# The first feed-forward matrix by seven products a block, its output through DRAM, the second matrix in four groups

## The reference

```
h = h + jnp.concatenate([y_rw, y_fox], axis=-1) @ w_out[i]     # 2048 x 2048
u = rmsnorm(h, norm_mlp[i])
h = h + jnp.square(jax.nn.relu(u @ w_ff1[i])) @ w_ff2[i]       # 2048 x 8192, 8192 x 2048
gate = jax.nn.sigmoid(rmsnorm(h, norm_ple[i]) @ w_ple_gate[i])
```

## Time and profile before

| stretch, us | what | PE busy | DVE busy | ACT busy | POOL busy |
|---|---|---|---|---|---|
| 1008 to 1095 | output projection, second half | 87.0 | 49.3 | 35.1 | 23.6 |
| 1095 to 2488 | the two feed-forward matrices | 1392.9 | 494.4 | 331.4 | 22.7 |
| whole span 2702.8 | | 2625.3 (97%) | 1232.4 (46%) | 896.8 (33%) | 192.4 (7%) |

### The profile page before, as it was taken

One profiled execution on the slowest core, in us unless ns is written; L12 is line 12 of the kernel. 1 busy time (PEld: TensorE's weight loads), 2 busy tenths in 40 slices (PEclk: granted clock), 3 DMA queues, 4 the chain that ended last, 5 costly groups with the idle time before them and its releaser, 6 DMA issues.

```text
span 2702.8 us, 45881 instructions
## 1 busy us (share of the span) xinstructions
PE 2625.3 (97%) x17810; PEld 2130.0 (79%) x17810; DVE 1232.4 (46%) x1638; ACT 896.8 (33%) x1338; POOL 192.4 (7%) x219
## 2 busy tenths in 40 slices
PE   7999999999688999999999999999999999999998
PEld 5777777777577678888888888888888888888887
DVE  5566676666644555443223442234422344334443
ACT  4443444444456324222122221222212122233333
POOL 0000000000233002000000000000000000011100
PEclk9999999999899999999999999999999999999999
DMA  7555444555523333333333333333333333333333
GB/s 201 152 153 162 141 141 143 164 162 149 189 87 105 112 99 95 99 100 94 94 100 93 101 94 95 99 93 101 93 96 98 94 100 93 98 96 107 95 97 105
DMA packets 524569, 310.26 MB, mean 115 GB/s; under 512 B 56501, under 2 KB 500903, under 8 KB 523495
## 3 DMA queue, kind: packets, MB, share of 16 engines
q1 hardware_dynamic: 475063, 265.15, 34.3%
q0 software_dynamic: 9264, 31.04, 3.3%
q10 hardware_dynamic: 40192, 13.40, 1.8%
HBM read 273.24 MB, written 36.31 MB: 115 GB/s over the span
## 4 chain that ended last, share of the span: by engine, by line
issue 53%; PE 35%; DVE 4%; ACT 3%; DMA 2%; POOL 1%; SPq 1%; POOLq 0%; DVEq 0%; ACTq 0%
PE acc L578 7%; PE acc L580 7%; PE acc L579 7%; PE acc L985 2%; PE acc L987 2%; PE acc L986 2%; ACT w_hi L1147 1%; POOL sumsq L2126 1%; PE bank L766 1%; PE acc L776 1%; PE bank L776 1%; DVE pr L1710 1%; PE bank L795 1%; DVE mx L1712 1%; PE bank L786 1%
## 5 line engine op out<-in xcount | busy, mean ns | idle before, releaser
L1581 DVE TENSOR_TENSOR w_lo<-w_raw,w_hi 128x1024 fp32r<-128x1024 f32 x420 | 521.5, 1242 | 1111.3 <-ACT w_hi L1147 1110.4
L1147 ACT ACTIVATE w_hi<-w_raw 128x1024 fp32r<-128x1024 f32 x420 | 444.5, 1058 | 1149.3 <-PE acc L580 1111.7
L578 PE MATMUL acc<-a_hi,w_hi 128*128 128x512 f32 x1824 | 719.9, 395 | 2.2 <-DVE w_lo L1581 2.1
L580 PE MATMUL acc<-a_hi,w_lo 128*128 128x512 f32 x1824 | 711.0, 390 | 0.0
L579 PE MATMUL acc<-a_lo,w_hi 128*128 128x512 f32 x1824 | 710.8, 390 | 0.0
L578 PE MATMUL acc<-b_hi,w_hi 128*128 128x512 f32 x1280 | 498.4, 389 | 0.0
L579 PE MATMUL acc<-b_lo,w_hi 128*128 128x512 f32 x1280 | 497.9, 389 | 0.0
L580 PE MATMUL acc<-b_hi,w_lo 128*128 128x512 f32 x1280 | 497.9, 389 | 0.0
L578 PEld LDWEIGHTS acc<-a_hi,w_hi 128*128 128x128 f32 x1824 | 342.8, 188 | 98.0 <-issue 22.4
L580 PEld LDWEIGHTS acc<-a_hi,w_lo 128*128 128x128 f32 x1824 | 342.8, 188 | 72.0
L579 PEld LDWEIGHTS acc<-a_lo,w_hi 128*128 128x128 f32 x1824 | 343.0, 188 | 71.6 <-issue 1.9
(11 more groups left out here) (297 smaller groups left out, 2032.9 us busy)
## 6 DMA issues: line engine op xcount, KB each, us to landing
w_raw<-in_w_ff SPq DMA_DIRECT2D x256, 512.0 KB, 4.0
w_raw<-in_w_in SPq DMA_DIRECT2D x100, 512.0 KB, 3.8
w_raw<-in_w_out SPq DMA_DIRECT2D x32, 512.0 KB, 4.1
w_raw<-in_w_ple_gate SPq DMA_DIRECT2D x32, 512.0 KB, 4.0
z_d<-ev POOLq DMA_DIRECT2D x50, 256.0 KB, 3.5
x_c<-ab_d SPq DMA_DIRECT2D x8, 1024.0 KB, 4.9
ab_d<-ab ACTq DMA_DIRECT2D x7, 1024.0 KB, 7.2
x_t<-ab_d SPq DMA_DIRECT2D x9, 512.0 KB, 3.6
```

Source lines behind the costliest of these rows:

```text
L578: mm(dst, wh, hi[:, kt, :], start=kt == 0, stop=False)
L580: last = mm(dst, wl, hi[:, kt, :], start=False, stop=kt == KT - 1)
L1147: A(w_hi[:, s, :, :], w_raw[:, s, :, :], ACT.Copy).then_inc(sg("w_hi_ready"), 1)
L1581: V.tensor_tensor(w_lo[:, s, :, 0:width], w_raw[:, s, :, 0:width], w_hi[:, s, :, 0:width].bitcast(F32), ALU.subtract).then_inc(sg("w_split ...
```

## The change

The first matrix (2048 x 8192) is cut into blocks of two by two: the input features in even and odd tiles of 128 (a = 0, 1), the tokens in two halves of 256, the hidden features in pairs of tiles of 128. Such a block product is made with seven products instead of eight. For that

- the normed input is kept as seven combinations (`mix`: a11, a12, s4, s1, s3, s2, a22, where s1 to s4 are sums of the four quarters), each of 256 tokens with high and low part side by side in one row of 512;
- of the weights the three blocks b11, b21, b22 and the four sums t1, t3, t2, t4 are used; GpSimd makes the sums, 1024 elements on each partition (`sum_weights`);
- a product is eight steps of two matmuls: w_hi with the row of 512 (high and low at once), w_lo with the 256 columns of the high part. VectorE reads the bank adding its two halves (`take_product`, a reduction), and adds up the seven results to the two output tiles;
- weights have four slots in place of two, and all seven other PSUM banks hold products;
- a finished pair of hidden tiles is squared by ScalarE and stored to DRAM (`hid_d`), 512 KB; `h` is stored too and reloaded after the first matrix, since `mix` takes its place;
- then the second matrix runs alone, in four groups of 16 tiles, each over a quarter of the hidden features; the next quarter is loaded and split during the group before.

32 pairs take the place of 64 tiles. The split of the input for the seven combinations is made in the output projection's second half: four 256-element sums of each pair of tiles on GpSimd, three copies on ScalarE, three residues on VectorE.

```diff
@@ TensorE
-            tiles(M_FF, 2, b_hi, b_lo, ready=2 * KT, beside=lambda u: spread_sumsq(1) if u == 1 else None)
-            tiles(M_FF + 2, KT - 2, b_hi, b_lo)
-            tiles(M_FF + KT, KT, a_hi, a_lo, ready=3 * KT)
-            with pe.Fori(0, FG - 1) as g:
-                tiles(M_FF + 2 * KT, KT, b_hi, b_lo, outer=g * (2 * KT))
-                tiles(M_FF + 3 * KT, KT, a_hi, a_lo, ready=g * KT + 4 * KT, outer=g * (2 * KT))
+            def seven_products(i, p, first=False):
+                for u in range(UNITS):
+                    wh, wl = slots[slot_of[u]]
+                    dst = product_banks[u]
+                    pe.wait_ge(sg("w_split"), i * UNITS + (FIRST + UNITS * p + u + 3))
...
+                    elif u % 2 == 0:
+                        pe.wait_ge(sg("products_taken"), i * 4 + (past("products_taken") + 4 * p - 3 + u // 2))
+                    for j in range(UK):
...
+                        mm(dst[:, :], wh[:, j, :], mixed(u, j), start=j == 0, stop=False, skip_group_check=True)
+                        last = mm(dst[:, 0:HT], wl[:, j, :], mixed(u, j)[:, 0:HT], start=False, stop=j == NJ, skip_group_check=True)
+                    last.then_inc(sg("unit_done"), 1)
...
+            seven_products(0, 0, first=True)
+            with pe.Fori(0, PAIRS - 1) as i:
+                seven_products(i, 1)
...
+            gemm(acc[0][:, :], *streams[0], Z_ODD + 2 * M_FF2, by_pair=2 * KT)
...
+            gemm(acc[1][:, :], *streams[0], Z_ODD + 2 * M_FF2 + 2)
+            tiles(M_FF2 + 2, KT - 2, *streams[0])
+            for g in range(1, FG):
+                tiles(M_FF2 + g * KT, KT, *streams[g % 2], ready=2 * KT + g * KT)
@@ SyncE
+            for q in range(4):
+                load_staged(q)
...
+            second_units(0, 0, 0)
+            for q in range(4, UK):
+                load_staged(q)
+            sp.wait_ge(sg("relu_ready"), past("relu_ready") + PAIRS)
+            sp.wait_ge(sg("hidden_stored"), past("hidden_stored") + 16 * PAIRS)
+            second_units(0, 0, 1)
+            stage_hidden(1, 0)
@@ VectorE
+            def product_lo(i, p, u):
+                dve.wait_ge(sg("w_hi_ready"), i * UNITS + (FIRST + UNITS * p + u + 1))
+                hi, lo = slots[slot_of[u]]
+                V.tensor_tensor(lo, weights_of[u], hi.bitcast(F32), ALU.subtract).then_inc(sg("w_split"), 1)
+            def take_product(dst, u):
+                return V.reduce_sum(dst, product_banks[u].rearrange("p (a t) -> p t a", a=2), AX.X)
...
+            def sums_4(i, p):
+                await_product(i, p, 6)
...
+                take_product(pq[1], 6).then_inc(sg("products_taken"), 1)
+                taken(i, p, 4)
+                then(V.tensor_tensor(ev[:, :, HT:T], pq[3][:, None, :].broadcast_to([P, 2, HT]), tile_sums[:, 1:3, :], ALU.add))
...
+                V.scalar_tensor_tensor(sq[:, :, :], ev[:, :, :], 0.0, rstd[:, None, :].broadcast_to([P, 2, T]), ALU.max, ALU.mult).then_inc(
+                    sg("relu_ready"), 1)
@@ GpSimd
+            def sum_weights(i, p):
+                b11, b12 = parts[:, 0, :, 0:P], parts[:, 0, :, P:]
+                b21, b22 = parts[:, 1, :, 0:P], parts[:, 1, :, P:]
+                t1, t3, t2, t4 = (tsum[:, n, :, :] for n in range(4))
+                def room(n):
+                    if p:
+                        pool.wait_ge(sg("w_split"), i * UNITS + (FIRST + UNITS * (p - 1) + n + 6))
...
+                G.tensor_tensor(t1, b12, b11, ALU.subtract).then_inc(sg("weight_sums_made"), 1)
...
+                G.tensor_tensor(t3, b22, b12, ALU.subtract).then_inc(sg("weight_sums_made"), 1)
...
+                G.tensor_tensor(t2, b22, t1, ALU.subtract).then_inc(sg("weight_sums_made"), 1)
...
+                G.tensor_tensor(t4, b21, t2, ALU.subtract).then_inc(sg("weight_sums_made"), 1)
```

More of the change, by code:

```diff
@@ L110, in sg @@
     def sg(name):
+        name = AGAIN[name][0] if name in AGAIN else name
         if name not in sems:
@@ L521, in _ @@
                     unit(b, w_out_v[:, 0:UK, bass.ds(i * (2 * P) + b * P, P)], i * 2 + (Z_ODD + 2 * M_OUT + KT + b))
[L522 to L530, removed]
+            ff1_parts = w_ff1.rearrange("l (k a p) n -> p (l a) k n", p=P, a=2)
@@ new lines, in _ @@
+            second_units(0, 0, 0)
[5 more added lines that the diff above has]
+            stage_hidden(1, 0)
+            for g in range(FG):
+                i0 = 1 if g == 0 else 0
+                with sp.Fori(0, KT // 2 - i0) as i:
+                    second_units(g, i, 0, i0)
+                    if g < FG - 1:
+                        stage_hidden(g + 1, i, i0)
+                    second_units(g, i, 1, i0)
@@ L1484, in _, with scale_tile @@
                     what(n)
[L1485 to L1492 removed]
+            def scale_tile(i, f0, b):
+                f = i * 2 + (f0 + b) if not isinstance(i, int) else f0 + b
+                act.wait_ge(sg("h_ready"), f + (KT + 1))
+                act.wait_ge(sg("mix_split"), i * 3 + (past("mix_split") + 3 * (f0 // 2)))
+                A(ev[:, b:b + 1, :], h[:, bass.ds(f, 1), :], ACT.Copy, scale=pc("norm_mlp", f)).then_inc(sg("tile_scaled"), 1)
@@ new lines, in _ @@
+            product_hi(0, 0, 0, first=True)
+            product_hi(0, 0, 1, first=True)
+            scale_tile(0, 2 * NJ, 1)
+            mix_his(0, NJ, 0)
+            product_hi(0, 0, 2, first=True)
+            square_tile(0, 2 * NJ, 1)
+            mix_his(0, NJ, 1)
+            mix_his(0, NJ, 2)
+            for u in range(3, UNITS):
+                product_hi(0, 0, u, first=True)
+            root(1)
+            with act.Fori(0, PAIRS - 2) as i:
+                for u in range(5):
+                    product_hi(i, 1, u)
+                square_hidden(i, 0)
+                for u in range(5, UNITS):
+                    product_hi(i, 1, u)
@@ L1510, in prepare @@
+                return body
+            for g in range(FG - 1):
+                stage(M_FF2 + g * KT, KT, body=next_hidden(g + 1))
+            stage(M_GATE - KT, KT, body=lambda i, b: fold(g_hi_all, "norm_ple", 2 * i + b, 2 * i + (b + 2 * KT), b))
             def prepare():
@@ new lines, in _, with to_last_lo @@
+            sums_76(0, 0)
+            product_lo(0, 1, 1)
+            def to_last_lo(i, p, last):
+                product_lo(i, p, 2)
+                product_lo(i, p, 3)
+                last()
+                product_lo(i, p, 4)
+                sums_12(i, p)
+                product_lo(i, p, 5)
+                product_lo(i, p, 6)
+            to_last_lo(0, 1, lambda: sums_4(0, 0))
+            with dve.Fori(0, PAIRS - 2) as i:
+                end = chained(i, 2)
+                sums_35(i, 1)
+                product_lo(i, 2, 0)
+                sums_76(i, 1)
+                product_lo(i, 2, 1)
+                to_last_lo(i, 2, lambda: sums_4(i, 1))
@@ L2240, in _ @@
+            sum_weights(0, 0)
+            with pool.Fori(0, PAIRS - 1) as i:
+                sum_weights(i, 1)
+            pool.wait_ge(sg("unit_done"), FIRST + 2 + UNITS * PAIRS)
+            for n in range(2):
+                pool.dma_start(h2[:, n * UK:(n + 1) * UK, :], h_v[:, n * UK:(n + 1) * UK, :]).then_inc(sg(f"h2_landed{n}"), 16)
+            for n in (2, 3):
                 sums(n)
```

439 lines of the change are left out of this document (353 added, 86 removed).

## The result

The changed kernel takes 2775.05 us (median of four runs, 2773.11 to 2777.12) where the kernel before takes 2704.4 in the same session: ratio 1.0258, 95% interval 1.0244 to 1.0273, 70 us slower. The forecast was 2765 us, range 2695 to 2830. The profiled execution has a span of 2773.8 us, 71.0 more than before.

The account below looks back on a forecast made before the run. VectorE and GpSimd, excluding each other at the SBUF port, were to bound the first matrix at 22.6 us a pair. -696.4 + 723.2 + 14 + 8 + 13 = +61.8 us on 2702.8 gave 2765 us, range 2695 to 2830.

Parts of the forecast that it names:

- likeliest case: Whole kernel: VectorE and GpSimd exclude each other, pair 22.6 us, total 2765 us, own range 2735 to 2800; chance 0.62.
- TensorE 19.4 us a pair as a floor: First matrix: seven products of 2.78 us make a 19.4 us pair, 75 us less in all if all else hides.
- A: Rival, first matrix: GpSimd's sums hide, TensorE stays the bound, pair 19.4 us, total 2650 us; chance 0.13.
- B: Rival, first matrix: narrow matmul doesn't halve because of its weight load, pair 24.8 us, total 2832 us; chance 0.06.
- D: Rival, first matrix: phases fall well, pair about 20.6 us, total within some 10 us of today; chance 0.06.
- The port, 6.3 us a pair: First matrix: of GpSimd's 9.6 us of sums 3.3 are covered; 6.3 add to VectorE's 16.3, pair 22.6 us.
- residues with a mean near 1.9 us: Sign of being right, first matrix: VectorE's weight residues have a mean near 1.9 us instead of 1.24.
- Rival C: First matrix: GpSimd keeps the port over consecutive sums while VectorE waits, pair 24.1 us, total 2824 us; chance 0.13.
- 8 was booked: First pair of the first matrix: weight sums start late, 8 us over an ordinary pair, ends 3 and 15.
- Projection, 14 us: Output projection's second half: chain of 12.9 us against TensorE's 10.9, 2.0 us booked seven times, ends 0 and 28.
- Handover, 13 us: Start of second matrix: late second-tile weights, wait 10.1 us, some 3 before the first tile; ends 5 and 20.
- Reloading the rows lies beside that: Handover to the second matrix: reloading rows, 5.9 us a megabyte, 2 MB first, lies beside the other waits.

Follow-up runs that it names:

- run 1: Changed kernel with GpSimd's four weight sums cut to 8 elements instead of 1024 from the second pair on; 2686.7 us, ratio 0.9931 to the kernel before.
- run 4: Changed kernel with three 256-column matmuls a step, VectorE copying 256 elements from the bank instead of reducing 512; 2747.97 us, ratio 1.0159 to the kernel before.
- run 7: Changed kernel with the second matrix's second weight tile requested before the wait for the last hidden pair's store; 2769.37 us, ratio 1.0239 to the kernel before.
- run 8: Run 7 with the reload of h issued later and VectorE waiting for it only at the first addition; 2765.23 us, ratio 1.0224 to the kernel before.
- run 5: Run 4 with VectorE adding straight from the product banks, weight sums kept on GpSimd; 2695.41 us, ratio 0.9961 to the kernel before.
- run 3: Changed kernel with the four weight sums made by VectorE instead of GpSimd from the second pair on; 2738.9 us, ratio 1.0126 to the kernel before.
- run 9: Changed kernel with ScalarE's weight copies ahead of scaling and mixing in the output projection's second half; 2763.95 us, ratio 1.0219 to the kernel before.
- run 6: Run 5 with the weight sums made by VectorE from the second pair on; 2695.26 us, ratio 0.9963 to the kernel before.
- run 2: Changed kernel with each weight sum replaced by two GpSimd fills of 1024 elements from the second pair on; 2685.31 us, ratio 0.9926 to the kernel before.

## Why the prediction was right

Its likeliest case came true, by its mechanism; that the pair agrees so closely, and the total within 10 us, is in part luck, as the steps show:

- **TensorE 19.4 us a pair as a floor.** The wide matmul starts a narrow one after 233 ns, the narrow one the next after 117, where 227 and 120 were taken. With nothing in its way (run 1) a pair takes 19.79 us. Rivals A, B and D are out: A needed the sums to hide, B a narrow matmul of 215 ns, D a pair of 20.6 us.
- **The port, 6.3 us a pair.** From the groups above: three residues (1.968 - 1.223), one L2347 (2.666 - 0.693), one L2320 (1.537 - 0.425), one L2329 (1.185 - 0.426) make 2.2 + 2.0 + 1.1 + 0.8 = 6.1 us of waiting a pair. Own work 16.3 was forecast, 22.56 - 6.1 = 16.5 measured, 0.3 of it idle. A sum that met nothing took 2.40 us, as taken from the rows, not 2.2. The pair of 22.6 was met to 0.04 us. What was wrong is where it waits: "residues with a mean near 1.9 us" holds for three of seven, and there as the mean of one of 3.4 and two of 1.2; 3.9 us of the 6.1 sit on additions of 256 and 512 elements, which I had not named. The cover was placed wrongly too. The forecast had reads of PSUM beside the four sums for 0.6, 1.2, 0 and 1.2 us; in the trace it is 0.2 (t1), 1.2 (t3), 1.4 (t2) and 0 (t4). Errors of over 1 us cancel, 3.0 against 2.8: that is luck. And the place can matter: in run 4 the same sums beside shorter reads cost more than before.
- **Rival C's mechanism is real, and its price shows only at the start.** In the first pair all four sums are ready to run one behind the other:

```profile
1120.90 2.36 POOL L2668 TENSOR_TENSOR tsum<-parts 128x1024 f32<-128x1024 f32 x1
1122.08 7.88 DVE L2296 TENSOR_TENSOR w_lo<-tsum,w_hi 128x1024 fp32r<-128x1024 f32 x2 [3.69 <-ACT w_hi L1677]
1123.21 2.35 POOL L2671 TENSOR_TENSOR tsum<-parts,tsum 128x1024 f32<-128x1024 f32 x1
1125.72 3.15 POOL L2674 TENSOR_TENSOR tsum<-parts,tsum 128x1024 f32<-128x1024 f32 x1 [0.17 <-POOL tsum L2671]
```

  Two residues, 2.4 us of work, take 7.88: VectorE asks during the sum of 1120.90 and does not get in ahead of that of 1123.21, only behind it, at 1125.6. The first pair is 34.4 - 22.6 = 11.8 us over an ordinary one, where 8 was booked (bounds 3 and 15); how much of that is C's was not measured. In the steady pairs C's 24.1 us don't come, but the argument against it ("the four sums mostly await one residue each") holds for two sums of four. The first awaits its load (L2665, 204.4 us of idle time ended by `parts`), and the last awaits nothing: L2674 starts 0.08 us after L2671 ends, in every pair. VectorE's small addition (1500.42) gets its turn between them; the residue behind it waits for the whole of the second sum, and this is the 3.4 us residue.
- **Projection, 14 us.** Seven waits of 2.2 to 2.4 us, 17 with the matmuls' own restart.
- **Handover, 13 us.** Waits of 11.5 (10.1 forecast) and 3.4 (3 forecast), 0.7 ahead of it, and 3.2 that the forecast lacks: the 12 matmuls behind the long wait start every 427 ns instead of 227 (2.4 us), at a mean granted clock of 0.74 in that window, and the rest are restarts. In all 18.8 us, near the upper bound of 20. (The expectation of run 7 counts 16 such matmuls; the trace shows 12.) "Reloading the rows lies beside that" was wrong: runs 7 and 8 show it in the way of weights and hidden rows, a term that was costed at nothing.
- **Sum.** 35.7 (first matrix) + 17 + 18.8 = 71.5 us, where the spans differ by 71.0; forecast 61.8. Of the 10 us between, 3 are the projection, 6 the handover and 1 the first matrix, in which the first pair is 3.8 above its term and the other 31 together 2.9 below (their mean is 22.51). The edges were sized too low by a fifth to a third.

## What to carry to other kernels

Before work is moved to an idle engine, add up what the two engines cannot do at the same time: VectorE instructions with two SBUF operands plus everything on GpSimd that reads SBUF, against the time that the bounding engine leaves. The sum is a lower bound for the time of a turn, and the order of the list comes on top. Here it was 21.0 us against 19.4, and the pair took 22.56; in run 4 it was still 21.0, and the pair took 21.8. In run 5, by the same count (residues 8.0, two additions of two SBUF operands 0.66, the scaling 1.14, the sums 9.6), it is 19.4 against 20.16, and the sums are hidden. Cutting VectorE's own reads and additions gained 80 us with the sums left on GpSimd (run 5), moving the sums alone 36 (run 3), and moving them on top of run 5 nothing. And where each wait is ended by an instruction that stood in a list behind something unrelated, as in the projection, exchanging entries of the list is worth trying first: it gained 11 us in run 9.

## What the runs showed of the chip beyond this

- GpSimd's fill of 1024 elements (0.955 us) leaves VectorE's two-operand instructions at 1.22 us; its sum of as many (2.4 us) blocks them.
- Matmuls of 256 columns in a row start every 120 ns, with the weight loads busy without a gap (runs 5 and 6); between wide ones the next starts after 117.
- After 11.5 us without work TensorE's clock was granted at 1.2 GHz for 12 matmuls (427 ns a matmul of 512 columns), then at 2.4 GHz again. Shorter waits can do it too. In the changed kernel the wait of 2.2 us that ends at 1109.52 is followed by 3.4 us at 1.2 GHz (640 ns for a wide and a narrow matmul, elsewhere 350), and the waits of 7.0 and 3.5 us, inside and behind the first pair, by some 3 us each; the first pair's window has a clock of 0.85; the six waits like it before 1109.5 are not. In run 1 three of the first six are (clock 0.51 from 1030.8 to 1034.0), and the next wait is then 0.6 to 0.8 us instead of 2.2. The ends of the waits stay 13.4 us apart: the slow matmuls took the place of waiting and cost nothing there. What decides between the two the runs don't show.
- The same wide and narrow step took 347 ns in the mean in the profiled execution of run 2 and 353 in run 1 (medians 344 and 350). What sets this is open. Run 2 multiplies by zero weights in four of seven products, but the step is as short in the other three; and its slower executions, up to 22 us longer, left no trace.
